# An order of evictions, rotations and gatings on VectorE, and GpSimd's low halves in two instructions

## The reference

```python
h = rms_norm(x, pre_w);  proj = h @ w_in          # 5952 columns: a_q .. c_g
qa, ka = apply_rope(a_q), apply_rope(a_k);  y_a = diff_attention(qa, ka, a_v, ...)
qb, kb = apply_rope(b_q), apply_rope(b_k);  y_b = sliding_window_attention(qb, kb, b_v, sinks)
qc  = rms_norm(c_q,  q_norm_w)  @ w_uq             # rank 512 to 4 heads of 128 + 64
kvc = rms_norm(c_kv, kv_norm_w) @ w_ukv            # rank 512 to 4 heads of 128 + 128
y_c = causal_attention(qc with rope, kvc with rope(c_kr), ...)
y = concat([y_a, y_b, y_c]) * silu(concat([a_g, b_g, c_g]))
x = x + rms_norm(y @ w_out, post_w)
```

## Time and profile before

| | |
|---|---|
| median of three launches | 2959.74 us |
| the profiled execution | 2964.29 us |
| its span, first to last instruction | 2962.5 us |
| mean granted clock of TensorE | 0.96 |
| TensorE matmuls, busy | 2755.4 us, 93% |
| weight loads into TensorE | 2164.6 us, 73% |
| VectorE | 1551.7 us, 52% |
| GpSimd | 1075.9 us, 36% |
| ScalarE | 847.7 us, 29% |
| DMA | 90 GB/s over the span |

### The profile page before, as it was taken

The page is one execution under the profiler, slowest core; times in us unless marked ns, Lnnn a source line. Parts: engine busy times, 40 slices in busy tenths (PEclk is TensorE's granted clock), DMA queues, the critical chain, the costliest instruction groups (busy, mean ns, idle before and its releaser), DMA issues. The chain is left out here.

```text
span 2962.5 us, 33679 instructions
## 1 busy us (share of the span) xinstructions
PE 2755.4 (93%) x12638; PEld 2164.6 (73%) x12638; DVE 1551.7 (52%) x2088; ACT 847.7 (29%) x1374; POOL 1075.9 (36%) x432
## 2 busy tenths in 40 slices
PE   7989999999998999999998999788999988999996
PEld 5777877867786777787776788666666676788885
DVE  4553146367525743316547833847799685311524
ACT  4233214225313322312314521411222223322321
POOL 4432432421343543243342154332222333444541
PEclk9999999999998999999999999888999998999998
DMA  4332332321432423232221143231111322423331
GB/s 155 95 100 72 92 92 58 86 71 39 160 93 71 146 82 93 74 98 78 65 86 57 65 157 95 95 122 58 64 58 56 121 77 86 153 91 94 104 99 71
DMA packets 246196, 268.65 MB, mean 91 GB/s; under 512 B 20544, under 2 KB 237248, under 8 KB 243648
## 3 DMA queue, kind: packets, MB, share of 16 engines
q1 hardware_dynamic: 240512, 222.33, 25.3%
q10 hardware_dynamic: 5568, 44.74, 3.9%
HBM read 246.06 MB, written 20.97 MB: 90 GB/s over the span
## 5 line engine op out<-in xcount | busy, mean ns | idle before, releaser
L517 POOL TENSOR_TENSOR w_lo<-w_raw,w_hi 128x1024 fp32r<-128x1024 f32 x428 | 1075.7, 2517 | 1841.9 <-ACT w_hi L529 1841.7
L1652 PE MATMUL gemm_ps<-act_hi,w_hi 128*128 128x512 f32 x2848 | 1149.1, 403 | 111.3 <-DVE tiles L906 42.6
L1653 PE MATMUL gemm_ps<-act_lo,w_hi 128*128 128x512 f32 x2848 | 1124.5, 395 | 0.0
L1654 PE MATMUL gemm_ps<-act_hi,w_lo 128*128 128x512 f32 x2848 | 1123.3, 394 | 0.0
L529 ACT CAST w_hi<-w_raw 128x1024 fp32r<-128x1024 f32 x428 | 448.0, 1050 | 1561.2 <-PE gemm_ps L1654 1391.8
L1652 PEld LDWEIGHTS gemm_ps<-act_hi,w_hi 128*128 128x128 f32 x2848 | 544.3, 191 | 263.5 <-issue 119.1
L1654 PEld LDWEIGHTS gemm_ps<-act_hi,w_lo 128*128 128x128 f32 x2848 | 543.8, 191 | 117.7
L1653 PEld LDWEIGHTS gemm_ps<-act_lo,w_hi 128*128 128x128 f32 x2848 | 544.8, 191 | 113.4 <-issue 4.3
L906 DVE TENSOR_TENSOR tiles<-gemm_ps,rstd 128x512 f32<-128x512 f32 (+1 forms) x58 | 39.2, 688 | 257.5 <-PE gemm_ps L1654 254.1
L1310 DVE COPY tiles<-gemm_ps 128x512 f32 x32 | 22.2, 692 | 210.8 <-PE gemm_ps L1654 210.3
L1603 DVE TENSOR_TENSOR tiles<-gemm_ps,att 128x512 f32<-128x512 f32 x16 | 11.0, 690 | 141.5 <-PE gemm_ps L1654 141.5
(11 more groups left out here) (380 smaller groups left out, 3144.8 us busy)
## 6 DMA issues: line engine op xcount, KB each, us to landing
w_raw<-in_w_in_dram SPq DMA_DIRECT2D x248, 512.0 KB
w_raw<-in_w_out_dram SPq DMA_DIRECT2D x96, 512.0 KB
w_raw<-in_w_ple_gate_dram SPq DMA_DIRECT2D x32, 512.0 KB
gate_scratch<-att ACTq DMA_DIRECT2D x16, 512.0 KB, 3.6
x_scratch<-tiles ACTq DMA_DIRECT2D x4, 2048.0 KB, 8.3
att<-x_scratch ACTq DMA_DIRECT2D x2, 4096.0 KB, 12.6
w_raw<-in_w_glu_dram SPq DMA_DIRECT2D x32, 256.0 KB
tiles<-in_x_dram ACTq DMA_DIRECT2D x4, 1024.0 KB, 10.6
```

The lines of the kernel that those rows point to most:

```text
L517: pool.tensor_tensor(w_lo[:, s], w_raw[:, s], w_hi[:, s].bitcast(F32), ALU.subtract).then_inc(wlo_done, 1)
L1652: pe.matmul(ps, left_hi, right_hi, start=first, stop=False, skip_group_check=True)
L1653: pe.matmul(ps, left_hi, right_lo, start=False, stop=False, skip_group_check=True)
L1654: return pe.matmul(ps, left_lo, right_hi, start=False, stop=last, skip_group_check=True)
```

## The change

It moves evictions on VectorE in front of other work at four places, and cuts GpSimd's instruction.

- cq's `rms` and `latent` come behind the eviction of ckv's first round; ScalarE's square root for them comes one unit of splits later (`through(("ckv", l), 4)`).
- In front of ukv's first eviction stand the second `gate_take` and one rotation; the second gating and the two other rotations come behind it.
- In bq the eviction of the second round comes in front of the rotation of `tiles[:, 6]`.
- In attention B the two rounds of gates are taken at steps 8 and 16, before at 9 and 17; ScalarE's tanh moves with them, and in attention B the multiplications onto y.
- GpSimd makes a unit's low half in two instructions of 512 columns with one signal behind the second.

```diff
-        GATES_AT = {br: {9: 0, 18 if br != "B" else 17: 1} for br in "CAB"}
+        GATES_AT = {br: {9: 0, 18: 1} if br != "B" else {8: 0, 16: 1} for br in "CAB"}
...
-                    pool.tensor_tensor(w_lo[:, s], w_raw[:, s], w_hi[:, s].bitcast(F32),
-                                       ALU.subtract).then_inc(wlo_done, 1)
+                    for k in range(0, UK, 2):
+                        ins = pool.tensor_tensor(w_lo[:, s, k:k + 2], w_raw[:, s, k:k + 2],
+                                                 w_hi[:, s, k:k + 2].bitcast(F32), ALU.subtract)
+                    ins.then_inc(wlo_done, 1)
...
-                through(("ckv", l), 3)
+                through(("ckv", l), 4)
                 root(f"cq{l}")
...
-                rms(f"cq{l}", 512)
-                latent(l, 0, 12, "qn")
                 for r in range(2):
                     for f in range(2):
                         round_done(("ckv", l), 4 * r + 3, f)
                         take(f, tiles[:, 2 * r + f])
                     if r == 0:
+                        rms(f"cq{l}", 512)
+                        latent(l, 0, 12, "qn")
                         dve.wait_ge(rcol_tp, l + 1)
...
-                for r in range(2):
-                    gate_take(g + r, ("bg1", l), r)
-                    gate_end(g + r)
-                rope(l, "C", [tiles[:, 9], tiles[:, 10], tiles[:, 8]])
+                gate_take(g, ("bg1", l), 0)
+                gate_end(g)
+                gate_take(g + 1, ("bg1", l), 1)
+                rope(l, "C", [tiles[:, 9]])
                 dve.wait_ge(lat_ready, 8 * l + 8)
                 for r in range(2):
                     for f in range(2):
                         round_done(("ukv", l), r, f)
                         take(f, tiles[:, 2 * r + f], None)
+                    if r == 0:
+                        gate_end(g + 1)
+                        rope(l, "C", [tiles[:, 10], tiles[:, 8]], 1)
...
+                bq_take(1)
                 rope(l, "B", [tiles[:, 6]], 3)
-                bq_take(1)
```

## The result

The changed kernel takes 2892.9 us (median of four runs, 2891.1 to 2895.6), the kernel before 2960.1 in four runs beside it: a ratio of 0.9777, with a 95% interval of 0.9760 to 0.9793. It is faster by 67 us. The prediction said 2912 with a low end of 2898, so the direction and most of the places were right, and the size was 19 us short, 5 us outside the range.

A forecast was written before the change was run, and what follows sets the result against it. It took TensorE's waits for VectorE, chiefly evictions, and the slow clock behind each stall as the bound. Four reorderings and GpSimd's halved instruction summed to -48.1 us: 2959.7 to 2911.6, said as 2912, range 2898 to 2934.

The forecast's parts named there:

- B: Second gating and two rotations moved behind ukv's first eviction: no stall before ukv's second round, 17.8 us saved over both layers.
- C: Bq's second eviction in front of a rotation: stall of 4.66 us cut to 0.6, 12.1 us saved over both layers.
- D: Attention B's gates at steps 8 and 16: 13.0 us saved at step 8, 3.0 us lost at step 16.
- A: Cq's norm behind ckv's first eviction: 7.8 us saved in layer 1, 3.5 us lost in layer 0.
- step E: GpSimd's low half in two instructions: 10.4 us gained, 6.5 us lost before x1 and at pairs, together 3.9 us saved.
- The later gate at step 16: Attention B: ScalarE's tanh of both banks delays the copy that item 15's transposes wait for, 3.0 us lost.
- Layer 0's tables: Trigonometric tables delay ckv's second eviction to 131.5 to 133; TensorE stands 7 to 8 us before uq, 3.5 us lost.
- Halves help everywhere: VectorE gets the port between GpSimd's halves and keeps it; some 20 meetings give 1 us each: 2893, chance 0.12.
- Stalls move: Half the savings at ukv, bq and attention B's gates come back as other waits, 20 us: 2932, chance 0.13.
- Clock: Slow stretches might have a reason other than the stalls, so only the idle goes: 2924, chance 0.10.
- slower case: A GpSimd half costs as much as a whole, felt first in the state steps: 3001, chance 0.04.
- no effect: The changed places are paced by something the trace hides: 2958, chance 0.03.

The follow-up runs named there:

- e5: Changed kernel with attention B's second round of gates at step 17 instead of 16: 2892.9 us, ratio 0.9774.
- e6: Changed kernel with lambda's two products before layer 0's tables and ckv's second round evicted between the sine's and cosine's tables: 2886.3 us, ratio 0.9758.
- e8: Changed kernel with bq's second eviction put back behind the rotation, a single run: 2908.0 us.
- e3: Changed kernel with GpSimd's low half in four instructions of 256 columns a unit: 2886.4 us, ratio 0.9757.
- e7: Changed kernel with GpSimd's low half in eight instructions of 128 columns a unit: 2888.3 us, ratio 0.9771.
- e1: Changed kernel with GpSimd's old single instruction of 1024 columns, so the new order alone: 2903.3 us, ratio 0.9818.
- e4: Kernel before, unchanged, run once more for a second profile, a single run: 2958.65 us.
- e2: Kernel before with only GpSimd's low half cut into two instructions of 512 columns: 2949.7 us, ratio 0.9975.

## Why the prediction was short

**Right.** B, C and step 8 of D, the large terms, came out within 0.6 us each, and A in layer 1 within 0.2: +17.2, +12.6, +13.2 and +8.0 by the ledger for 17.8, 12.1, 13.0 and 7.8. The rule behind them held, that a stall costs its idle and what its slow matmuls lose. For step 8 the agreement is in part luck: e5, with the same stall of 1.65 us there, is 3.2 us ahead of the changed kernel behind it, by the clock alone. The new stall before uq came in layer 0 only, though 5.4 us long for the 7 forecast, and a half takes 1.29 us for the 1.30 taken. The Trainium skill, "GPSIMD Engine Reference", section "Performance versus the Vector engine", had led to an estimate of 1.35 for it; the trace's 1.29 stands.

**Wrong.** What failed are sizes in the sum: step E, put at 3.9 us, measured 10.4, and the order, put at 44.2, measured 54.9. The 1.9 us that are left of the 19 are rounding and two medians of the kernel before, 2959.7 and 2958.2. Step E fails most, since it had the price at x1 and in the pairs too high and the slow matmuls at the post norms at nothing. Within the order, three terms were off, one of them a clock effect that no step held. All four went to the same side, and the range, which was built from rivals, was not wide enough for their sum. By the ledger, in the order of size:

- Step E, about 7 (6.5 by the medians). Of it, +4 at x1, where the prediction charged 4.0 for a later store of x_scratch and 0.2 was lost. The store is issued 1.5 us later after the additions' start (973.40 - 956.80 = 16.6, before 1001.75 - 986.62 = 15.1), as the step had it, but from its issue to the first eviction there are 8.1 us for 9.2. In the halves alone x1 did cost 2.4, and in e5, e6 and e8 it takes another 1.5 to 2.5 over the changed kernel, so the mechanism is there and the size was not. Another +2.3 at the post norms: the idle fell by 1.08 each, as said, and the slow matmuls behind it by as much again, which the step left out though A to D and the term for wo counted them. The +0.25 a place for some ten places did not show either: +0.7 for -2.5 in the state steps and behind x2. There the halves without the new order lose 6.5, so this part hangs on what meets what. Wo gave 2.4 less than forecast: in layer 1 its stall, 1.51 us in the kernel before, is gone with the order alone. So E's own error is a sum of errors of both signs.
- The later gate at step 16, 3.9, of which 3.0 was the charge for a longer stall. e5 settles that one: what one stall gained in length the next one lost.
- The clock at the start of attention B, 3.1, which no step held. A stall that the change does not touch lost its slow stretch in both layers. As far as any run shows this is luck: e6 has one of the stretches back and e8 both.
- Layer 0's tables, 2.4. TensorE finished at 125.3, as said, but VectorE evicted at 130.8, before the 131.5 to 133 of the step. In front of uq there also stood a small matmul for lambda (L1888), whose products VectorE makes behind the tables; the prediction had not named it, and e6 moves them too.

The working of part E states a rule for pairs alone. Of two VectorE instructions in a row it said that "each waits for a half, 2 x 1.30 against 2.40". In the rotations, where one unit meets two instructions, that came true, sign and size (VectorE's timeline, one rotation before and after):

```profile
613.80 2.54 DVE L983 TENSOR_TENSOR tiles<-tiles,cos_t 128x512 f32<-128x512 f32 x1
616.38 0.69 DVE L993 TENSOR_TENSOR tiles<-tiles,att 128x512 f32<-128x512 f32 x1
```

```profile
603.99 1.17 DVE L985 TENSOR_TENSOR tiles<-tiles,cos_t 128x512 f32<-128x512 f32 x1
605.20 1.66 DVE L995 TENSOR_TENSOR tiles<-tiles,att 128x512 f32<-128x512 f32 x1
```

By the medians of all rotations the product fell by 1.10 us and the addition behind it grew by 0.97. The rule can't be carried to longer rows of instructions with more units to come, and the prediction's words leave that open, though its term for x2 (2.8, measured 3.0) had it right. In the trace before, each of the long additions had waited for a whole unit (4.37, 3.31 and 2.76 us). So the right comparison there is one wait per VectorE instruction, before and after, and a smaller piece shortens each. The Trainium skill, "SBUF — State Buffer", section "Who interferes with whom", gives the exclusive lock on the shared pair, and the traces agree: VectorE's addition of 961.25 ends at 964.51, and GpSimd's half of 962.33 at 965.66, 1.15 us behind it, for its own 1.29: nothing of it ran beside the addition but the start. What the prediction added to it, that a second half blocks VectorE once more, holds only where VectorE has more instructions ready than GpSimd had units, as in the rotations. e3 shows the rule's use, e7 its end: VectorE's busy time goes from 1563.8 us (e1) to 1514.5, 1421.6 and 1355.7 with two, four and eight pieces, GpSimd's from 1079.6 to 1202.4, 1402.4 and 1721.0.

**The rivals.** "Halves help everywhere", at 2893, names the measured time, but it is not what happened: it wanted some 20 us from the halves, and they give 8.5 alone and 10.4 on top. "Stalls move" was right for one term, the gate, where it worked in the change's favour. "Clock" fell: behind the places of B and C, where the stalls are gone, the granted clock is 1.00, and the slow stretches came back with C's stall in e8. The slower case fell with the half's 1.29 us, and "no effect" with the result.

**What stays open.** Why the halves cost 6.5 us behind x2 and in the state steps in the old order and nothing in the new one. Against e4, TensorE in e2 idles 3.6 us more there and has the half clock for 6.8 us more, so idle and clock share the loss about evenly. But the first profile of the kernel before is itself 3 us slower there than e4, so a good part of it may be the difference between two profiles of one kernel. Nor does any run say what sets the clock's fall behind a short stall.

## What to carry to other kernels

Compare kernels with the same list of matmuls by the start of the n-th one: it turns a difference of 67 us into terms that can be held against a sum, and shows which were never in it. Where GpSimd and VectorE share work with operands in SBUF, cut GpSimd's instruction until its unit's own length begins to be waited for; in these traces a meeting costs the piece that is met, and the cut gains nothing where VectorE has as many instructions waiting as there are pieces. When a delayed instruction is charged, look at the next wait of the same engine before it is added to the sum, and count the slow matmuls behind every stall or behind none.

## What was not expected of the hardware

The same stall of 1.8 to 2.0 us was followed by a granted clock of 0.66 in the kernel before and of 1.00 in the changed one. Two executions of one kernel differed by 5.7 us of span with nearly the same stalls. And 3424 instructions of 128 columns on GpSimd, 0.46 us each, leave the kernel no slower than 856 of 512 do (2888.3 against 2892.9), although GpSimd is busy 519 us longer.
